# Attention in a two-block transformer kernel: the probabilities multiplied by the reciprocal of their sum on GpSimd instead of VectorE

## The chip, the cores and the metric

The kernel runs on one core of a Trainium2 chip. The metric is the device time of one execution in microseconds. The kernel before was timed three times; the median is 2486.6 us. The profile is of one more execution, with a time of its own.

## What is computed

Everything is in float32. A first block has two layers over 256 latent tokens and 256 context tokens of width 1024: modulated norm, one wide input projection, attention with two kinds of heads (six of latent attention with a low-rank key and value, six with a sliding window and a sink), a short convolution, an output projection, and 16 experts. The second block has two layers over the 256 latent tokens with four mixers side by side (stick-breaking attention, RWKV-7, block attention called moba, HGRN-2), gates and a feed-forward part. What matters here is the softmax of the attentions:

```
def sink_softmax(scores, sink):
    s_sink = jnp.broadcast_to(sink..., scores.shape[:-1] + (1,))
    p = jax.nn.softmax(jnp.concatenate([scores, s_sink], axis=-1), axis=-1)
    return p[..., :-1]
...
    s = (einsum('bqhd,bkhd->bhqk', qn, kn) + einsum('bqhr,bkr->bhqk', qr, kr)) * MLA_SCALE
    p = jax.nn.softmax(s, axis=-1)
    return jnp.einsum('bhqk,bkhd->bqhd', p, v)
```

In layer 0 both token streams attend (12 heads each); in layer 1 the latent one only. Latent queries see 512 keys (context and latent), context queries see 256. In each layer of the second block moba has four heads with 256 keys, all causal.

## The kernel before, in words

Five engines run programs of their own, in order, and meet at semaphores. `Signals.mark` counts an event on a semaphore of the engine that makes it, and `at` gives the value that another engine must wait for; the program is built twice, so that the second pass knows all values from the first. TensorE writes to eight PSUM banks, which `take` hands out in turn. Weights stream through a ring of three slots in SBUF, filled by SyncE; a slot is loaded again when TensorE has read it.

All attentions use four functions. A head has 256 queries in two halves j = 0, 1 of 128 rows, so each score tile is 128 x 512 or 128 x 256 (`nk` keys). Buffers alternate by head (`i % 2`). For each head:

- TensorE, `attend_tensor`: `scores(i + 1)`, then `between(i)`, which is filler from elsewhere (in layer 0 the modulation rows of layer 1, L491; in moba the projections of the next columns, L274; nothing in the context stage and in layer 1), then for every second head `values` of two finished heads, then `turned(i - 1)`: it waits for the probabilities of head i - 1 and transposes them (L645), half j = 0 and then j = 1.
- VectorE, `attend_vector`: `stats(i)`: mask if there is one (L679), row maximum (L680), three small operations (L683 to L685); then `normalise(i - 1)`: sum plus sink (L691), reciprocal (L692), the two multiplications of the probabilities (L695), and then `out_turned(i - 1, 1)`, the copy of the second half of the transposed probabilities from PSUM (L610), which waits for TensorE.
- ScalarE, `attend_scalar`: the exponentials with their sums (L720), the sink's exponential (L723), the copy of the first half of the transposed probabilities and of the attended values (L615).
- GpSimd has no part in it. Its program is `sum_pool` (sums of squares for the norms, L551), one memset (L1287) and, in the second block, `rwkv_pool` (L1750, L1755), after each layer's attentions.

Of the kernel before, what the change touches and what calls it, by code (L numbers as in the profile page):

```python
# [16 lines left out]
ALU = mybir.AluOpType  # L17
# [10 lines left out]
L = 2  # L28
# [170 lines left out]
def program(nc, A, out, book):  # L199
    ctx = ExitStack()  # L200
    with ctx:
# [7 lines left out]
        gpsimd = Signals("gpsimd", nc, ctx, book)  # L209
# [13 lines left out]
        stat = sb("stat", 160)  # L223
# [302 lines left out]
        def link(dve, ins):  # L526

            ins.then_inc(*vector.mark("chain"))
            dve.wait_ge(*vector.now("chain"))
# [16 lines left out]
        def sum_pool(pool, T, tag):  # L546

            pool.wait_ge(*scalar.at("squares", tag, 0))
            for k in range(1, KD - 1):
                pool.wait_ge(*scalar.at("squares", tag, k))  # L550
                nc.gpsimd.tensor_tensor(squared(T, tag, 0), squared(T, tag, 0), squared(T, tag, k), ALU.add).then_inc(*gpsimd.mark("summed", tag))  # L551
                pool.wait_ge(*gpsimd.now("summed"))
# [77 lines left out]
        def attend_tensor(pe, heads, prob, probT, tag, between=None):  # L630


            def scores(i):
                q, keys, nk = heads[i][0:3]
                for j in range(2):
                    b = take(pe, "scores", tag, i, j)
                    mm(b[:, 0:nk], q(j), keys, 0, 1).then_inc(*tensor.mark("scores", tag, i, j))

            def turned(i):
                n = heads[i][2] // P  # L640
                for j in range(2):
                    pe.wait_ge(*vector.at("probs", tag, i, j))
                    b = take(pe, "turned_probs", tag, i, j)
                    for k in range(n):
                        last = PE.transpose(b[:, k * P:(k + 1) * P], prob[i % 2][:, j, k * P:(k + 1) * P], ident)  # L645
                    last.then_inc(*tensor.mark("turned_probs", tag, i, j))

            def values(i):

                b = take(pe, "attended", tag, i)  # L650
                for hd in (i, i + 1):
                    for j in range(2):
                        pe.wait_ge(*got("turned_probs", tag, hd, j))
                n = heads[i][2] // P
                for k in range(n):
                    for hd in (i, i + 1):
                        last = mm(b[heads[hd][4], 0:S], heads[hd][3](k), probT[hd % 2][:, k, :], k, n)
                last.then_inc(*tensor.mark("attended", tag, i))

            scores(0)  # L660
            for i in range(len(heads) + 2):
                if i + 1 < len(heads):
                    scores(i + 1)
                if between and i <= len(heads):
                    between(i)
                if i >= 3 and i % 2:
                    values(i - 3)
                if 1 <= i <= len(heads):
                    turned(i - 1)

        def attend_vector(dve, heads, prob, probT, tag, between=None):
            def stats(i):
                nk, mask, sink, scale = heads[i][2], heads[i][6], heads[i][7], heads[i][8]
                mx, nm, es = (stat[:, 32 + 8 * (i % 2) + 2 * n:34 + 8 * (i % 2) + 2 * n] for n in range(3))
                for j in range(2):
                    dve.wait_ge(*tensor.at("scores", tag, i, j))
                    b = bank("scores", tag, i, j)
                    if mask is not None:
                        link(dve, V.tensor_tensor(b[:, 0:S], b[:, 0:S], mask[:, j, :], ALU.add))  # L679
                    V.reduce_max(mx[:, j:j + 1], b[:, 0:nk], AX).then_inc(*vector.mark("chain"))  # L680
                dve.wait_ge(*vector.now("chain"))
                sk = sink.broadcast_to((P, 2))
                link(dve, V.scalar_tensor_tensor(mx, mx, scale, sk, ALU.mult, ALU.max))  # L683
                V.tensor_scalar(nm, mx, -1.0, None, ALU.mult).then_inc(*vector.mark("chain"))
                V.tensor_tensor(es, sk, mx, ALU.subtract).then_inc(*vector.mark("maxima", tag, i))  # L685

            def normalise(i):
                nk = heads[i][2]
                es, sm = (stat[:, 32 + 8 * (i % 2) + 2 * n:34 + 8 * (i % 2) + 2 * n] for n in (2, 3))
                dve.wait_ge(*scalar.at("sink", tag, i))  # L690
                link(dve, V.tensor_tensor(sm, sm, es, ALU.add))  # L691
                link(dve, V.reciprocal(sm, sm))  # L692
                for j in range(2):
                    pr = prob[i % 2][:, j, 0:nk]
                    V.tensor_scalar(pr, pr, sm[:, j:j + 1], None, ALU.mult).then_inc(*vector.mark("probs", tag, i, j))  # L695
                out_turned(i, 1)

            def out_turned(i, j):
                n = heads[i][2] // P
                out_vector(dve, probT[i % 2][:, 0:n, j * P:(j + 1) * P],  # L700
                           bank("turned_probs", tag, i, j)[:, 0:n * P].rearrange("p (k q) -> p k q", k=n),
                           "turned_probs", tag, i, j)

            for i in range(len(heads) + 1):
                if i < len(heads):
                    stats(i)
                if between:
                    between(i)
                if i:
                    normalise(i - 1)  # L710

        def attend_scalar(act, heads, prob, probT, tag, between=None):
            def exps(i):
# [691 lines left out]
        def moba_heads():  # L1405
            causal = C("causal").rearrange("p (a t) -> p a t", a=2)
            heads = []
            for hd in range(4):
                parts, c = sl_of(hd), hd // 2
                heads.append((lambda j, parts=parts, c=c: raw_m[parts, c, j * P:(j + 1) * P], raw_m[parts, 2 + c, :], S,  # L1410
                              lambda k, hd=hd: vt_m[:, k, 64 * hd:64 * hd + 64], parts, ys[2][:, c, :],
                              causal, C("no_sink"), HEAD_SCALE))
            return heads
# [323 lines left out]
        def rwkv_pool(pool, l):  # L1737

            for s in (tensor, scalar, vector):
                value = s.closed(("group1", l))  # L1740
                if value:
                    pool.wait_ge(*value)
            pool.wait_ge(*vector.at("pairs", l, "NT", 1))
            for lev in range(LEVELS):
                if lev:
                    pool.wait_ge(*tensor.at("NT_T", l, lev - 1, 1))
                if lev == 1:
                    pool.wait_ge(level_masked, LEVELS * l + 1)
                    for par in range(2):
                        nc.gpsimd.tensor_tensor(TT[:, par * 512:(par + 1) * 512].rearrange("p (u t) -> p u t", u=4),  # L1750
                                                NL[par].rearrange("p (u t) -> p u t", u=4),
                                                ident.unsqueeze(1).broadcast_to((P, 4, P)), ALU.add).then_inc(identity_added, 1)
                    pool.wait_ge(identity_added, 2 * l + 2)
                for par in range(2):
                    last = nc.gpsimd.tensor_tensor(NL[par].rearrange("p (u t) -> p u t", u=4),  # L1755
                                                   NT[:, par * 512:(par + 1) * 512].rearrange("p (u t) -> p u t", u=4),
                                                   C("levels")[:, lev * P:(lev + 1) * P].unsqueeze(1).broadcast_to((P, 4, P)), ALU.mult)
                last.then_inc(level_masked, 1)
# [477 lines left out]
        with nc.Block() as block:  # L2236
# [84 lines left out]
            @block.gpsimd  # L2321
            def _(pool):
                sum_pool(pool, T2, ("n1", 0))
                for l in range(L):
                    sum_pool(pool, T2 if l < L - 1 else S, ("n2", l))
                    moe_pool(pool, l)
                    sum_pool(pool, T2 if l < L - 1 else S, after_moe(l))
                sum_pool(pool, S, ("m1", 0))
                pool.wait_ge(second_loaded, 16 * len(second_list))
                for l in range(L):  # L2330
                    rwkv_pool(pool, l)
                    sum_pool(pool, S, ("m2", l))
                    sum_pool(pool, S, after_ffn(l))
# [27 lines left out]
```

## Time and profile before

| | |
|---|---|
| median of 3 runs | 2486.6 us (2482.49 to 2492.38) |
| profiled execution | 2477.03 us, its span 2475.3 us |
| TensorE matmul busy | 2245.7 us (91%) |
| VectorE busy | 721.1 us (29%) |
| ScalarE busy | 452.8 us (18%) |
| GpSimd busy | 99.0 us (4%) |
| mean granted TensorE clock | 0.969 |

The span runs from the first to the last instruction of the profiled execution. Busy shares are means over stages that have different limits; TensorE's busy time contains modelled ends of pipelined matmuls. The attention stages lie at 229 to 308 us (latent tokens, layer 0), 310 to 353 (context tokens, layer 0), 827 to 902 (latent tokens, layer 1), and near 1290 to 1311 and 1908 to 1931 (moba).

### The profile page before, as it was taken

The page shows a single profiled execution, that of the slowest core. Times are in us where ns is not written, and L with a number is a line of the kernel's source. Part 1 is how long each engine was busy: PE and PEld are TensorE (multiplying, and loading weights), DVE is VectorE, ACT ScalarE, POOL GpSimd, SP SyncE. Part 2 cuts the span into 40 slices and gives each one's busy share as a digit, 9 for nine tenths or more (in the row PEclk, how much of TensorE's full clock was granted, in tenths as well). Part 3 has the DMA queues.
Part 4 walks back from the last instruction along what each step waited for, and adds up shares of the span by engine and source line. Part 5 has one row for each costly group of instructions (what it writes and reads, how often), then busy time and mean ns, then how long its engine had stood idle before and what let it go on. Part 6 is the DMA issues. An engine that isn't in the chain of part 4 may idle for free.

```text
span 2475.3 us, 26852 instructions
## 1 busy us (share of the span) xinstructions
PE 2245.7 (91%) x11495; PEld 1620.3 (65%) x11495; DVE 721.1 (29%) x1521; ACT 452.8 (18%) x973; POOL 99.0 (4%) x97
## 2 busy tenths in 40 slices
PE   5999889999879888888898999999999899999998
PEld 2334344755456465444587888888888778788887
DVE  2106542223232633111345441400014544131001
ACT  3002332111120322000122312100002331120000
POOL 1000001000010000000100110000000011000000
PEclk8999979999999889999999999999999999999999
DMA  9533901599933004999542213334543211244352
GB/s 327 191 135 143 377 1 68 225 409 415 424 147 132 1 34 197 425 422 424 194 140 102 103 44 127 137 136 136 141 146 139 103 69 68 102 147 145 134 137 84
DMA packets 172887, 435.00 MB, mean 176 GB/s; under 512 B 6202, under 2 KB 64482, under 8 KB 156130
## 3 DMA queue, kind: packets, MB, share of 16 engines
q1 hardware_dynamic: 171632, 430.91, 46.8%
q10 hardware_dynamic: 1138, 2.38, 0.3%
q8 instruction: 92, 1.51, 0.3%
q14 instruction: 25, 0.20, 0.0%
HBM read 432.23 MB, written 1.05 MB: 175 GB/s over the span
## 4 chain that ended last, share of the span: by engine, by line
PE 71%; DMA 15%; DVE 8%; ACT 3%; issue 1%; POOL 1%; SPq 0%; ACTq 0%; POOLq 0%; DVEq 0%
PE bank L274 68%; DMA ring<-in_exp_w_up 13%; PE bank L645 1%; DMA ring<-in_w_in 1%; DVE rstd L575 1%; POOL arena L551 1%; PE bank L491 1%; DMA ring<-in_ada_w 1%; DVE stat L680 1%; DVE arena L610 1%; DMA arena<-in_x 1%; DVE bank L625 0%; ACT h L570 0%; ACT arena L615 0%; DVE arena L626 0%
## 5 line engine op out<-in xcount | busy, mean ns | idle before, releaser
L274 PE MATMUL bank<-h,ring 128*128 128x256 f32 (+1 forms) x4064 | 1003.7, 407 | 26.8 <-DMA ring<-in_w_in 10.8
L274 PEld LDWEIGHTS bank<-h,ring 128*128 128x128 f32 x4064 | 771.5, 191 | 245.0 <-issue 125.2
L274 PE MATMUL bank<-arena 128*128 128x128 f32 (+14 forms) x1616 | 314.1, 392 | 47.6 <-ACT arena L615 12.9
L274 PEld LDWEIGHTS bank<-arena 128*128 128x128 f32 (+5 forms) x1616 | 212.5, 206 | 132.8 <-issue 87.3
L274 PE MATMUL bank<-ring,arena 128*64 128x256 f32 x2048 | 234.1, 382 | 48.9 <-DMA ring<-in_exp_w_up 34.1
L274 PE MATMUL bank<-arena,ring 128*128 128x256 f32 x1216 | 264.1, 380 | 6.7 <-DVE arena L2096 3.9
L274 PEld LDWEIGHTS bank<-arena,ring 128*128 128x128 f32 x1216 | 230.7, 190 | 40.1 <-DVE arena L2096 4.7
L274 PEld LDWEIGHTS bank<-ring,arena 128*64 128x64 f32 x2048 | 142.9, 137 | 151.4 <-DMA ring<-in_exp_w_up 47.2
L615 ACT ACTIVATE arena<-bank 128x256 f32<-128x256 f32 (+4 forms) x269 | 119.0, 459 | 637.4 <-PE bank L274 615.0
L610 DVE COPY arena<-bank 128x256 f32<-128x256 f32 (+8 forms) x122 | 65.2, 536 | 389.9 <-PE bank L274 298.8
L551 POOL TENSOR_TENSOR arena<-arena 128x256 f32<-128x256 f32 (+1 forms) x60 | 53.5, 891 | 1877.0 <-ACT arena L544 1875.4
L274 PE MATMUL bank<-ring,h 128*64 128x512 f32 x512 | 116.9, 598 | 3.6 <-DVE h L610 2.4
L544 ACT ACTIVATE arena<-x 128x256 f32<-128x256 f32 (+1 forms) x80 | 36.8, 478 | 341.0 <-DVE x L2175 161.9
L2172 DVE TENSOR_TENSOR arena<-arena,bank 128x512 f32<-128x512 f32 x22 | 15.1, 687 | 285.6 <-PE bank L274 285.6
L1125 DVE TENSOR_TENSOR h<-h,bank 128x256 f32<-128x256 f32 x32 | 13.5, 421 | 254.0 <-PE bank L274 254.0
L274 PE MATMUL bank<-h,arena 128*128 128x256 f32 (+2 forms) x256 | 72.4, 404 | 8.0 <-ACT h L570 5.6
L274 PEld LDWEIGHTS bank<-ring,h 128*64 128x64 f32 x512 | 35.7, 136 | 66.5 <-issue 59.7
L274 PE MATMUL bank<-arena,cst 128*128 128x256 f32 (+1 forms) x132 | 47.8, 492 | 30.6 <-POOL arena L551 21.7
L1144 ACT ACTIVATE arena<-bank 32x512 f32<-32x512 f32 x48 | 28.1, 586 | 242.3 <-PE bank L274 242.1
L615 ACT ACTIVATE h<-bank 128x256 f32<-128x256 f32 (+1 forms) x76 | 30.4, 400 | 210.0 <-PE bank L274 187.1
L720 ACT ACTIVATE arena<-bank,stat 128x512 f32<-128x512 f32 (+1 forms) x88 | 51.1, 586 | 89.9 <-DVE stat L685 89.9
L645 PE MATMUL bank<-cst,arena 128*128 128x128 f32 x272 | 44.1, 302 | 23.1 <-DVE arena L695 21.5
(273 smaller groups left out, 1356.4 us busy)
## 6 DMA issues: line engine op xcount, KB each, us to landing
ring<-in_w_in SPq DMA_DIRECT2D x32, 2048.0 KB, 7.9
ring<-in_exp_w_gate SPq DMA_DIRECT2D x32, 2048.0 KB, 11.0
ring<-in_exp_w_up SPq DMA_DIRECT2D x32, 2048.0 KB, 11.0
ring<-in_exp_w_down SPq DMA_DIRECT2D x32, 2048.0 KB, 10.3
ring<-in_ada_w SPq DMA_DIRECT2D x24, 2048.0 KB, 12.3
ring<-in_w_ffn_down SPq DMA_DIRECT2D x16, 1408.0 KB, 7.0
ring<-in_w_ffn_gate SPq DMA_DIRECT2D x10, 2048.0 KB, 7.8
ring<-in_w_ffn_up SPq DMA_DIRECT2D x10, 2048.0 KB, 7.8
```

Of the source, the lines that this page charges most:

```text
L274: return PE.matmul(o, lhsT, rhs, start=(k == 0), stop=(k == n - 1))
L491: last = PE.matmul(banks[7][g:g + 32, :], cond32[:, k, o:o + 32], w[:, k, :], start=(r == 0 and k < 4), stop=(r == n - 1 and k >= 4))
L544: SC.activation(squared(T, tag, k), x[:, k, 0:T], ACT.Square).then_inc(*scalar.mark("squares", tag, k))
L551: nc.gpsimd.tensor_tensor(squared(T, tag, 0), squared(T, tag, 0), squared(T, tag, k), ALU.add).then_inc(*gpsimd.mark("summed", tag))
L575: link(dve, V.reciprocal(rstd[:, 0:T], rstd[:, 0:T]))
L610: V.tensor_copy(dst, src).then_inc(*vector.mark(*key))
L615: SC.activation(dst, src, func, **kw).then_inc(*scalar.mark(*key))
L645: last = PE.transpose(b[:, k * P:(k + 1) * P], prob[i % 2][:, j, k * P:(k + 1) * P], ident)
L680: V.reduce_max(mx[:, j:j + 1], b[:, 0:nk], AX).then_inc(*vector.mark("chain"))
L720: SC.activation(prob[i % 2][:, j, 0:nk], bank("scores", tag, i, j)[:, 0:nk], ACT.Exp, bias=nm[:, j:j + 1], scale=scale, accum_out=sm[:, j: ...
L1144: last = SC.activation(yst[32 * q:32 * q + 32, g % 2, s, 0:512], bank("expert_down", l, e)[s * CAP:(s + 1) * CAP, :], ACT.Copy)
L2172: V.tensor_tensor(a, a, halves(bank("ffn_up", l, f)), ALU.mult).then_inc(*vector.mark("ffn_up", l, f))
```

## The change

The multiplications of the probabilities leave `normalise` on VectorE, whose reciprocal now marks the event `inverse`. A new function `attend_pool` on GpSimd waits for it and makes the two multiplications of the head. TensorE's transposes wait for GpSimd's event. In GpSimd's program the function stands in front of the sums of norm 2 in the first block, and in front of `rwkv_pool` in the second.

```diff
@@ attend_tensor
-                    pe.wait_ge(*vector.at("probs", tag, i, j))
+                    pe.wait_ge(*gpsimd.at("probs", tag, i, j))
@@ attend_vector
             def normalise(i):
-                nk = heads[i][2]
                 es, sm = (stat[...] for n in (2, 3))
                 dve.wait_ge(*scalar.at("sink", tag, i))
                 link(dve, V.tensor_tensor(sm, sm, es, ALU.add))
-                link(dve, V.reciprocal(sm, sm))
-                for j in range(2):
-                    pr = prob[i % 2][:, j, 0:nk]
-                    V.tensor_scalar(pr, pr, sm[:, j:j + 1], None, ALU.mult).then_inc(*vector.mark("probs", tag, i, j))
+                V.reciprocal(sm, sm).then_inc(*vector.mark("inverse", tag, i))
                 out_turned(i, 1)
@@ new
+        def attend_pool(pool, heads, prob, tag):
+            for i in range(len(heads)):
+                nk = heads[i][2]
+                pool.wait_ge(*vector.at("inverse", tag, i))
+                for j in range(2):
+                    pr, inverse = prob[i % 2][:, j, 0:nk], stat[:, 38 + 8 * (i % 2) + j:39 + 8 * (i % 2) + j]
+                    nc.gpsimd.tensor_scalar(pr, pr, inverse, None, ALU.mult).then_inc(*gpsimd.mark("probs", tag, i, j))
@@ GpSimd's program
                 sum_pool(pool, T2, ("n1", 0))
                 for l in range(L):
+                    for s, tag in enumerate(("lat", "ctx")[0:2 if l < L - 1 else 1]):
+                        attend_pool(pool, head_list(l, s), prob1, (tag, l))
                     sum_pool(pool, T2 if l < L - 1 else S, ("n2", l))
                     moe_pool(pool, l)
...
                 for l in range(L):
+                    attend_pool(pool, moba_heads(), prob_m, ("moba", l))
                     rwkv_pool(pool, l)
```

## Rows read from the trace of the kernel before

**Rows 1.** Page: busy us, share, count; then the chain that ended last

```profile
PE 2245.7 (91%) x11495; PEld 1620.3 (65%) x11495; DVE 721.1 (29%) x1521; ACT 452.8 (18%) x973; POOL 99.0 (4%) x97
...
PE 71%; DMA 15%; DVE 8%; ACT 3%; issue 1%; POOL 1%; SPq 0%; ACTq 0%; POOLq 0%; DVEq 0%
```

**Rows 2.** Stretches: us, busy of PE, PEld, DVE, ACT, POOL, PEclk, DMA, GB/s

```profile
310.00:353.00 43.00, 33.21 (x144) 20.39 (x144) 28.32 (x120) 19.51 (x78) 0.00 (x0) 0.78 0.00 1
...
862.00:876.00 14.00, 11.74 (x43) 6.08 (x42) 8.52 (x24) 4.85 (x16) 0.00 (x0) 0.67 0.00 0
...
980.00:1180.00 200.00, 172.09 (x1174) 93.07 (x1172) 32.77 (x67) 15.65 (x34) 0.00 (x0) 1.00 1.01 424
```

**Rows 3.** TensorE's waits in 310:354, 825:905, 229:308: us in total, times, longest

```profile
PE bank L645 <- DVE arena L695: 8.1, 9, 1.4
...
PE bank L645 <- DVE arena L695: 11.7, 7, 2.3
...
PE bank L491 <- DMA ring<-in_ada_w: 2.4, 1, 2.4
```

**Rows 4.** Timeline, context stage: start us, duration us, engine, line, operation

```profile
334.48 0.17 DVE L692 RECIPROCAL stat<-stat 128x2 f32<-128x2 f32 x1
...
335.08 0.70 PE L645 MATMUL bank<-cst,arena 128*128 128x128 f32 x4 [0.23 <-DVE arena L695]
...
335.82 0.42 DVE L610 COPY arena<-bank 128x256 f32<-128x256 f32 x1 [0.53 <-PE bank L645]
...
337.48 0.17 DVE L692 RECIPROCAL stat<-stat 128x2 f32<-128x2 f32 x1
```

**Rows 5.** Timeline, layer 1's latent stage

```profile
838.34 0.17 DVE L692 RECIPROCAL stat<-stat 128x2 f32<-128x2 f32 x1
...
839.09 1.09 PE L645 MATMUL bank<-cst,arena 128*128 128x128 f32 x8 [1.52 <-DVE arena L695]
...
840.02 3.76 PE L274 MATMUL bank<-arena 96*128 96x512 f32 x20
...
840.22 0.69 DVE L610 COPY arena<-bank 128x512 f32<-128x512 f32 x1 [0.79 <-PE bank L645]
...
849.60 6.38 PE L274 MATMUL bank<-arena 64*128 64x512 f32 x19
```

**Rows 6.** Timeline, where GpSimd follows ScalarE, itself, and TensorE follows it

```profile
377.82 0.63 ACT L544 ACTIVATE arena<-x 128x512 f32<-128x512 f32 x1 [6.24 <-DVE x L941]
...
378.59 1.26 POOL L551 TENSOR_TENSOR arena<-arena 128x512 f32<-128x512 f32 x1 [5.58 <-ACT arena L544]
...
1209.47 5.02 POOL L551 TENSOR_TENSOR arena<-arena 128x256 f32<-128x256 f32 x6 [5.64 <-ACT arena L544]
...
1214.64 0.77 PE L274 MATMUL bank<-arena,cst 128*128 128x256 f32 x1 [5.28 <-POOL arena L551]
...
1356.62 1.27 POOL L1755 TENSOR_TENSOR arena<-arena,cst 128x512 f32<-128x512 f32 x1 [142.12 <-DVE arena L1832]
1357.85 1.27 POOL L1755 TENSOR_TENSOR rstd<-arena,cst 128x512 f32<-128x512 f32 x1
```

**Rows 7.** GpSimd's groups by form: shapes, count, busy us, mean ns, idle before

```profile
L551 POOL TENSOR_TENSOR arena<-arena 128x256 f32<-128x256 f32 x42 | 30.7, 731 | 1188.3 <-ACT arena L544 1187.5
...
L1287 POOL MEMSET arena<- 128x4096 f32 x1 | 3.5, 3511 | 3.5 <-PE bank L274 3.5
...
L2353 POOL MEMSET const-float32-0.0<- 128x1 f32 x1 | 0.1, 98 | 0.2 <-issue 0.2
```

**Rows 8.** Chain in order of time, layer 0: start us, us, what

```profile
266.09 17.15 DMA ring<-in_ada_w
```

**Rows 9.** Timeline, moba of the first mixer layer

```profile
1304.77 0.17 DVE L692 RECIPROCAL stat<-stat 128x2 f32<-128x2 f32 x1
...
1307.24 0.42 DVE L610 COPY arena<-bank 128x256 f32<-128x256 f32 x1 [1.65 <-PE bank L645]
```

## The prediction

> **What bounds the kernel now.** I read the page first. VectorE is busy for 29% of the span and GpSimd for 4%, and the chain of waits puts 71% on TensorE and 8% on VectorE [rows 1]. From that alone the move looks free: VectorE is not the bound and GpSimd has time. So the share is not what to look at, and I went to the stages that hold the edited lines. There are 44 heads in five stretches: 12 latent heads of layer 0 (229 to 308 us), 12 context heads (310 to 353), 12 latent heads of layer 1 (827 to 902), and four moba heads in each of two mixers (near 1290 to 1311 and 1908 to 1931). Then the stages one by one: in the context stage no DMA moves, TensorE is granted 0.78 of its clock and GpSimd is idle; in 14 us of layer 1's stage the same with 0.67 [rows 2]. The table of waits for these stages has the multiplications of L695 first: TensorE waited 8.1 us for them in the context stage and 11.7 us in layer 1's [rows 3].
>
> The timeline of the context stage shows why. It repeats every 3.00 us: reciprocal at 334.48, two multiplications behind it, transposes on TensorE at 335.08 to 335.78, VectorE's copy of them at 335.82, and right behind it the row maxima of the head after next and the next reciprocal, at 337.48 [rows 4]. VectorE is in order and its copy (out_turned) stands in front of the next head's statistics, so reciprocal, multiplication, transposes, copy and maxima form one ring. Whatever is added between reciprocal and copy is added to the ring; TensorE also resumes its scores and values only after the transposes, so the addition counts once, on both sides alike.
>
> **The change, part by part.** It takes 88 multiplications off VectorE (48 of 128x512, 40 of 128x256) and puts as many on GpSimd, with two new crossings between engines. What VectorE saves buys nothing: after the reciprocal its next instruction is the copy that waits for the very transposes, so it merely waits longer. That excludes a gain in these stages. No instruction of another kind is queued on GpSimd in the five stretches: its sums for n2, and rwkv_pool, come after them in its order as they do in time, so its queue delays nothing.
>
> Let *gap* be the time from the start of a head's reciprocal (L692) to the start of its copy (L610). For a head in the ring it is 1.34 us at 256 columns (334.48 to 335.82) and 1.88 at 512 (838.34 to 840.22) [rows 4, 5]. The new gap, if nothing hides it, is: reciprocal 0.17; crossing to GpSimd 0.15; two multiplications of d each, the second starting 0.04 before the first ends, as two unlinked GpSimd operations do at 1356.62 and 1357.85; crossing to TensorE 0.15; the second half of the transposes, 0.35 at 256 (half of 0.70) and 0.50 at 512 (half of 1.09, less the part that overlaps); 0.04 to the copy [rows 4, 5, 6]. The crossings are read where they stand now: ScalarE ends at 378.45 and GpSimd starts at 378.59, GpSimd ends at 1214.49 and TensorE starts at 1214.64 [rows 6]. Hence 0.82 + 2d at 256 columns and 0.97 + 2d at 512. The first multiplications of the pair let the first transposes start earlier, but the second pair ends last for every d above that half.
>
> What is d? No GpSimd operation of one tensor input is in the trace. From below there are memsets, which read nothing: 98 ns for one element and 3511 ns for 4096, so 0.83 ns an element, 0.31 us at 256 and 0.52 at 512. From above there are tensor_tensor operations, which read two: 0.73 us at 256 and 1.27 at 512 [rows 6, 7]. A multiplication by a per-partition scalar reads one, so I take the middle, 0.52 and 0.89 us; VectorE takes 0.35 and 0.48. New gaps: 1.86 at 256 (+0.52 on a ring head) and 2.75 at 512 (+0.87).
>
> Each head loses only what its present gap doesn't already hold. I read the 44 gaps off VectorE's timeline.
> Context, 12 heads: 7 at 1.34 or 1.35, the others 1.59, 1.76, 1.77, 1.98, 2.10. Loss 7 x 0.52 + 0.27 + 0.10 + 0.09 = 4.1 us.
> Layer 1, 12 heads: 7 at 1.87 or 1.88, then 2.17, 2.75, and three of 4.70 to 5.64, where TensorE's own work comes last. Loss 7 x 0.87 + 0.58 = 6.7.
> Layer 0, 12 heads: TensorE has the modulation rows as filler. Five heads have gaps of 3.29 to 7.26 and lose nothing, one has 1.88, six have 2.14 to 2.33. Two of those six (264.57, 276.81) lie in front of the load that TensorE waits for until 283.28: it was issued at 266.09 behind the second set of loads on SP and took 17.15 us, and TensorE stood still for 2.4 us at its end [rows 3, 8], so the 1.1 us that these two lose disappear in that wait. What comes before 258 does not, since the chunk's release, and with it SP's queue, moves along. Loss 1.2 before and 1.9 after: 3.0.
> Moba, 8 heads: gaps 2.47 to 4.92; the tightest is 1304.77 to 1307.24 [rows 9]. The cover is TensorE's 16 projection matmuls (3.7 us) between transposes. Even with d of 0.73 the new gap is 2.28. Loss 0. Without that filler it would be 0.5 us a head.
> The same sum at both ends: with memset prices 2.5 us (0.1 + 1.2 + 1.1), with tensor_tensor prices 29.4 (6.8 + 8.7 + 13.5, 0.4 of the gap before 283 included).
>
> What follows the stages neither returns nor multiplies this. Within them no more than three chunks of weights can be loaded ahead, so later loads shift with the work; the experts behind layer 1 run at 424 GB/s with all DMA engines busy [rows 2] and start their loads as the chunks before are used, so the delay passes to the end.
>
> Sum: 3.0 + 4.1 + 6.7 = +13.8 us. The profiled execution took 2477.0 us with a span of 2475.3, so it would become 2490.8; but it is 9.6 us under the median of the runs shown (2486.6), and on the median's footing the forecast is **2500.4 us**. I give that one.
>
> **The rivals.**
> *The multiplication runs at one element a cycle* (not slower). The memset slope of 0.83 ns an element with the fixed part of the tensor_tensor rows (2 x 0.73 - 1.27 = 0.2) gives d of 0.41 and 0.62, gaps of 1.64 and 2.21, and +4.9 us: 2491.5, no change that can be told. For it: the memset does hold that slope over 4096 elements. Against it: the only arithmetic on GpSimd in the trace needs 2.1 ns an element (0.54 us more for 256 elements more). It decides below 0.85 us for a 128x512 operation, where the sum falls under 12.4 us.
> The Trainium skill ("GPSIMD Engine Reference", § 4.1 Engine selection) has GpSimd about two times slower for two-input elementwise work and says "1-input is roughly line-rate"; the rival above is what this would make here, +4.9 where my middle gives +13.8. By that rule, then, nothing measurable changes. The trace has the two-input case alone, and shows nothing of the other.
> *The multiplication is as slow as tensor_tensor*: +29.4 us, 2516.0. For it: all GpSimd arithmetic here is so. Against it: one operand fewer to read.
> *The clock falls further.* TensorE is at its lower level for part of these stages already. At 849.60 a group of 19 score and value matmuls took 6.38 us where 20 took 3.76 at 840.02 [rows 5]. If the one such group before 849 also falls, that is +3.1, and I allow the context stage, whose groups are smaller, as much again. With the sum: +20, 2506.6. For it: the granted clock of 0.67 and 0.78 in the stages with the ring, against 1.00 among the experts [rows 2]. Against it: the pauses grow by under 1 us each.
> *It doesn't do what it says* would need the multiplications to stay on VectorE or another wait to hold the copy; the diff leaves no room for that, so it has no chance of its own.
>
> **How the numbers follow.** Forecast 0.40 (2493 to 2508 for itself), one element a cycle 0.27, as slow as two inputs 0.12, clock 0.14, something not seen 0.07. A measurement tells about 0.5%, 12.4 us, from no change, so slower begins at 2499. The forecast straddles that: 0.26 of its 0.40 above. With 0.12, 0.13 of the clock's and 0.01 of the rest, slower is 0.52; same 0.44; faster 0.04, all of it from the unseen, since no mechanism here gives time back. The range 2487 to 2514 holds both neighbouring cases and leaves out the very dear multiplication and the free one with a low run.
>
> **What would show each step right or wrong.** The duration of the GpSimd tensor_scalar rows: 0.5 and 0.9 us, or not. The ring of the context stage: 3.5 us instead of 3.0 between reciprocals. In the table of waits TensorE waits for GpSimd at L645, some 15 to 20 us more in total than it did for L695. VectorE's busy time falls by some 35 us (88 multiplications of 0.35 or 0.48), GpSimd's rises by about 64 (48 x 0.89 + 40 x 0.52), and neither matters. The moba stretches keep their length. The prediction is wrong if a 128x512 multiplication takes under 0.7 us, if the crossings are far from 0.15, or if TensorE's granted clock in the layer 1 stage moves by more than a tenth.

## The result: 58 us slower, and the profile after

The changed kernel takes 2545.7 us (median of 4 runs, 2537.6 to 2550.3) against 2488.0 for the kernel before, a ratio of 1.023 with a 95% interval of 1.0196 to 1.0263: +57.7 us where +13.8 was forecast, outside the range. Between the two profiled executions the difference is larger, 69.5 us (2546.6 and 2477.0), because the kernel before was profiled in one of its fastest runs. Where stages are compared below, it is the profiled executions that are compared.

The page of the changed kernel, its chain by engine and three of its groups (columns as before: busy us, mean ns of one, idle before and what ended it):

```profile
PE 70%; DMA 14%; DVE 8%; POOL 3%; ACT 3%; issue 1%; ACTq 0%; POOLq 0%; DVEq 0%
...
L551 POOL TENSOR_TENSOR arena<-arena 128x256 f32<-128x256 f32 (+1 forms) x60 | 53.5, 891 | 1377.1 <-ACT arena L544 1375.5
L715 POOL TENSOR_SCALAR arena<-arena,stat 128x512 f32<-128x512 f32 (+1 forms) x88 | 110.9, 1271 | 657.8 <-DVE stat L691 657.8
...
L645 PE MATMUL bank<-cst,arena 128*128 128x128 f32 x272 | 56.9, 343 | 52.2 <-POOL arena L715 51.7
```

GpSimd has gone from 1% of the chain [rows 1] to 3%, and TensorE's transposes (L645) now wait 51.7 us for it. Its own groups by form give the price that the prediction had to bound:

```profile
L715 POOL TENSOR_SCALAR arena<-arena,stat 128x512 f32<-128x512 f32 x48 | 74.4, 1562 | 431.2 <-DVE stat L691 431.2
L715 POOL TENSOR_SCALAR arena<-arena,stat 128x256 f32<-128x256 f32 x40 | 36.4, 922 | 226.5 <-DVE stat L691 226.5
```

1.56 and 0.92 us, above what was taken for the upper end (1.27 and 0.73). The timeline of the context stage answers to [rows 4]:

```profile
339.60 0.17 DVE L691 RECIPROCAL stat<-stat 128x2 f32<-128x2 f32 x1
339.86 1.82 POOL L715 TENSOR_SCALAR arena<-arena,stat 128x256 f32<-128x256 f32 x2 [12.23 <-DVE stat L691]
...
340.83 0.44 PE L645 MATMUL bank<-cst,arena 128*128 128x128 f32 x2 [1.27 <-POOL arena L715]
...
341.73 0.44 PE L645 MATMUL bank<-cst,arena 128*128 128x128 f32 x2 [0.46 <-POOL arena L715]
...
342.21 0.42 DVE L610 COPY arena<-bank 128x256 f32<-128x256 f32 x1 [2.45 <-PE bank L645]
...
343.87 0.17 DVE L691 RECIPROCAL stat<-stat 128x2 f32<-128x2 f32 x1
```

The gap from reciprocal to copy is 2.61 us (1.34 before), and the next reciprocal comes 4.27 us after the last one (3.00 before): the ring is as described, with another size. The table by stage (us, then busy of PE, PEld, DVE, ACT, POOL, granted clock, DMA, GB/s) shows a second thing; first the kernel before, then the changed one, for layer 0, the context tokens and layer 1:

```profile
235.00:304.00 69.00, 63.06 (x398) 27.48 (x397) 42.20 (x121) 25.40 (x73) 0.00 (x0) 0.97 1.05 381
315.00:351.00 36.00, 27.29 (x127) 15.95 (x125) 25.65 (x112) 17.97 (x72) 0.00 (x0) 0.83 0.00 1
834.00:898.00 64.00, 51.42 (x214) 26.73 (x212) 42.03 (x120) 25.11 (x72) 0.00 (x0) 0.79 0.00 1
```

```profile
236.00:329.00 93.00, 78.29 (x399) 30.14 (x397) 31.82 (x98) 25.79 (x73) 37.23 (x24) 0.81 0.84 300
340.00:392.00 52.00, 38.22 (x124) 20.30 (x124) 18.21 (x84) 18.16 (x72) 21.71 (x24) 0.62 0.00 1
877.00:964.00 87.00, 62.65 (x212) 31.26 (x212) 31.30 (x96) 25.41 (x72) 37.22 (x24) 0.66 0.00 0
```

The stages are 23, 16 and 23 us longer, which is 63 of the 69.5; the work behind them, which starts at the lower clock, makes 5 of the other 7, the time ahead of the first stage 1.0, and moba 0.4. TensorE's granted clock fell from 0.97, 0.83 and 0.79 to 0.81, 0.62 and 0.66. The fourth group of 16 modulation matmuls in layer 0 took 1.9 us and takes 3.6 us in the changed kernel, about twice as long, as at 1.2 instead of 2.4 GHz (timeline of layer 0, before and after):

```profile
245.02 1.92 PE L491 MATMUL bank<-ring,arena 128*32 128x512 f32 x16
```

```profile
249.62 3.64 PE L491 MATMUL bank<-ring,arena 128*32 128x512 f32 x16
```

### The profile page after: what moved, and what is told of

Read it like the earlier page. It is cut to its first block, busy times and chain, and to the rows that moved or that the text cites. A ratio compares the mean times of both kernels' runs of the same rounds, so it can differ in the third digit from the quotient of the medians.

```text
span 2544.8 us, 26855 instructions
## 1 busy us (share of the span) xinstructions
PE 2289.2 (90%) x11495; PEld 1635.6 (64%) x11495; DVE 687.9 (27%) x1433; ACT 453.9 (18%) x973; POOL 209.9 (8%) x185
## 4 chain that ended last, share of the span: by engine, by line
PE 70%; DMA 14%; DVE 8%; POOL 3%; ACT 3%; issue 1%; ACTq 0%; POOLq 0%; DVEq 0%
PE bank L274 67%; DMA ring<-in_exp_w_up 13%; POOL arena L715 2%; PE bank L645 1%; DVE stat L680 1%; PE bank L491 1%; DMA ring<-in_w_in 1%; DVE rstd L575 1%; POOL arena L551 1%; DVE arena L610 1%; DMA arena<-in_x 1%; DVE bank L625 0%; ACT h L570 0%; ACT arena L615 0%; DVE arena L626 0%
## 5 line engine op out<-in xcount | busy, mean ns | idle before, releaser
L274 PE MATMUL bank<-arena 128*128 128x128 f32 (+14 forms) x1616 | 333.0, 409 | 47.7 <-ACT arena L615 12.9
L274 PEld LDWEIGHTS bank<-arena 128*128 128x128 f32 (+5 forms) x1616 | 219.3, 213 | 143.7 <-issue 99.1
L274 PEld LDWEIGHTS bank<-ring,arena 128*64 128x64 f32 x2048 | 143.7, 138 | 152.8 <-DMA ring<-in_exp_w_up 47.9
L715 POOL TENSOR_SCALAR arena<-arena,stat 128x512 f32<-128x512 f32 (+1 forms) x88 | 110.9, 1271 | 657.8 <-DVE stat L691 657.8
L645 PE MATMUL bank<-cst,arena 128*128 128x128 f32 x272 | 56.9, 343 | 52.2 <-POOL arena L715 51.7
L544 ACT ACTIVATE arena<-x 128x256 f32<-128x256 f32 (+1 forms) x80 | 36.8, 478 | 343.5 <-DVE x L2180 161.9
L645 PEld LDWEIGHTS bank<-cst,arena 128*128 128x128 f32 x272 | 36.1, 169 | 85.8 <-POOL arena L715 81.0
```

What stands on the lines that cost most here:

```text
L274: return PE.matmul(o, lhsT, rhs, start=(k == 0), stop=(k == n - 1))
L544: SC.activation(squared(T, tag, k), x[:, k, 0:T], ACT.Square).then_inc(*scalar.mark("squares", tag, k))
L715: nc.gpsimd.tensor_scalar(pr, pr, inverse, None, ALU.mult).then_inc(*gpsimd.mark("probs", tag, i, j))
```

## The experiments

Two causes had to be told apart: the ring (each head pays what GpSimd adds between reciprocal and copy) and the clock (TensorE, idle for longer, runs slower where it does work). All differences are medians against the kernel before, run beside it on the same chip; the ratio's interval tells how far each can be trusted (0.001 is 2.5 us). This table has the length of each stage, from the start of its first reciprocal to the start of its last copy, and the granted clock in it, from the one profiled execution of each run; each experiment below refers to it. In runs 1 and 9 the code of these three stages is that of the kernel before. Its context stage takes 35.7, 37.1 and 36.8 us in the three profiles, and layer 1 64.2, 60.2 and 60.3: single stages differ by up to 4 us without any cause in the code.

| run | us against before | ratio (95%) | layer 0 | context | layer 1 |
|---|---|---|---|---|---|
| kernel before | | | 69.8, 0.97 | 35.7, 0.83 | 64.2, 0.79 |
| changed kernel | +57.7 | 1.023 (1.0196 to 1.0263) | 93.1, 0.81 | 52.0, 0.62 | 87.4, 0.66 |
| 1 moba only | -0.8 | 0.9988 (0.9969 to 1.0007) | 70.0, 0.97 | 37.1, 0.78 | 60.2, 0.83 |
| 2 crossing only | +6.3 | 1.003 (1.0008 to 1.0052) | 69.5, 0.97 | 42.6, 0.66 | 66.3, 0.79 |
| 3 half the columns | +23.3 | 1.0086 (1.0056 to 1.0115) | 70.6, 0.99 | 45.7, 0.66 | 76.6, 0.71 |
| 4 idle matmuls | +48.1 | 1.0182 (1.0147 to 1.0217) | 82.1, 0.96 | 51.6, 1.00 | 85.6, 0.90 |
| 5 fewer idle matmuls | +44.1 | 1.0174 (1.0139 to 1.0209) | 82.0, 0.96 | 51.0, 0.93 | 81.4, 0.90 |
| 6 late copy, GpSimd | -19.8 | 0.9924 (0.9894 to 0.9954) | 70.4, 0.96 | 28.7, 0.94 | 48.6, 0.89 |
| 7 late copy, VectorE | -26.5 | 0.9893 (0.9852 to 0.9934) | 70.4, 0.94 | 29.6, 0.88 | 47.9, 0.93 |
| 8 tensor_tensor form | +25.8 | 1.0108 (1.0076 to 1.0139) | 75.2, 0.93 | 46.3, 0.63 | 78.1, 0.69 |
| 10 late copy, tensor_tensor | -36.2 | 0.9843 (0.9817 to 0.9868) | 68.8, 0.97 | 24.7, 1.00 | 45.1, 0.92 |
| 11 before, idle matmuls | -11.3 | 0.9947 (0.9922 to 0.9972) | 69.7, 0.97 | 35.2, 0.97 | 56.1, 1.00 |
| 12 early maxima, GpSimd | +4.7 | 1.0013 (0.9994 to 1.0031) | 70.6, 0.96 | 42.8, 0.72 | 69.3, 0.76 |

**1. GpSimd multiplies in moba only.** In the first block VectorE keeps its multiplications, and GpSimd's part is taken out there.

```diff
...
-                    pe.wait_ge(*gpsimd.at("probs", tag, i, j))
+                    pe.wait_ge(*(gpsimd if tag[0] == "moba" else vector).at("probs", tag, i, j))
...
```

> Only the eight moba heads are multiplied on GpSimd; the first block multiplies on VectorE as before. Ring theory (each head loses what its gap between reciprocal and copy does not already hold): the tightest moba gap before is 2.47 us and the new one, with two 0.92 us multiplications, 2.61, so at most 0.1 us on each of four heads: +0.5 us over the kernel before. Rival, that GpSimd's work costs by itself (shared memory port, slower neighbours): 16 of 88 multiplications, a fifth of the 57.7 us, +8 to +12 us.

Measured: -0.8 us, no change. Sixteen operations of 0.92 us on GpSimd cost nothing where TensorE's projections lie between the transposes; the 8 to 12 us of the rival are outside the interval.

```profile
L721 POOL TENSOR_SCALAR arena<-arena,stat 128x256 f32<-128x256 f32 x16 | 14.6, 922 | 185.3 <-DVE stat L692 185.3
```

**2. The crossing alone.** GpSimd copies two numbers a row, and VectorE waits for that and multiplies itself; TensorE waits for VectorE.

```diff
...
                 V.reciprocal(sm, sm).then_inc(*vector.mark("inverse", tag, i))
+                dve.wait_ge(*gpsimd.at("probs", tag, i))
+                for j in range(2):
+                    pr = prob[i % 2][:, j, 0:heads[i][2]]
+                    V.tensor_scalar(pr, pr, stat[:, 104 + 2 * (i % 2) + j:105 + 2 * (i % 2) + j], None, ALU.mult)...
...
+                nc.gpsimd.tensor_copy(stat[:, 104 + 2 * (i % 2):106 + 2 * (i % 2)], stat[:, 38 + a:40 + a])...
```

> VectorE multiplies as before, but waits for a GpSimd copy of the two reciprocals (128x2) in between: two crossings and one tiny operation, no long GpSimd work. Ring theory: the gap grows by about 0.09 + 0.1 + 0.09 = 0.3 us, 15 heads pay it whole and some pay part: +4 to +6 us. Rival, that crossings between engines are what is dear: most of the 57.7 us, +30 or more.

Measured: +6.3 us (2 to 13 by the interval), at the upper edge of what the ring gives. In the stage table layer 0 is unchanged and layer 1 has 2 us more, which is within the spread, but the context stage has 7 and its clock fell from 0.83 to 0.66, below the 0.78 of run 1: the shortest gaps there are 1.59 us instead of 1.35, so about 0.24 us more of waiting a head went with the lower clock. Crossings are not what is dear.

**3. Half the columns.**

```diff
-                    pr, inverse = prob[i % 2][:, j, 0:nk], stat[...]
+                    pr, inverse = prob[i % 2][:, j, 0:nk // 2], stat[...]
```

> As the changed kernel, but GpSimd multiplies only the first half of the columns; the other half of the probabilities is left unscaled, so part of the computation is left out. With 2.5 ns an element (0.92 at 256, 1.56 at 512) the operations take 0.92 us for 512 keys and 0.60 for 256, close to the 0.89 and 0.52 of the prediction. Ring theory alone: gaps of 2.83 and 1.97, +16 us (3.4 + 5.2 + 7.4). Ring and clock: the granted clock of the attention stages falls too and adds to it, +20 to +30 us. If the loss were a matter of the count of GpSimd operations and not of their length: the whole 57.7 us.

Measured: +23.3 us, with 14 to 29 by the interval. That is in the range of ring and clock together, but the ring's 16 is inside it too. The run has nearly the prediction's own prices (0.92 and 0.60 us), and its context stage is 10.0 us longer than before where the ring's sum has 5.2, at a clock of 0.66 instead of 0.83; so it points to the clock beside the ring without proving it. What it does show is that the loss follows the length of the operation, not the number of operations.

**4. and 5. Idle matmuls in TensorE's wait, in the changed kernel**, first in run 4, then in run 5. keep_busy(pe, n) issues 2n matmuls of 128x256, which are 4n rows of the profile and take n us at full clock.

```diff
             def turned(i):
                 n = heads[i][2] // P
+                if tag[0] != "moba" and (tag != ("lat", 0) or i % 2):
+                    keep_busy(pe, 1 if tag == ("lat", 0) else 2)
                 for j in range(2):
                     pe.wait_ge(*gpsimd.at("probs", tag, i, j))
```

```diff
+                if tag[0] == "ctx" or tag[0] == "lat" and i % 2:
+                    keep_busy(pe, 2 if tag == ("lat", 1) else 1)
                 for j in range(2):
                     pe.wait_ge(*gpsimd.at("probs", tag, i, j))
```

> The changed kernel with idle matmuls on TensorE in front of its wait for the probabilities in the first block's attentions (four of 128x256 a head in the context stage and in layer 1, two on every second head in layer 0), in time in which it would stand still. Clock theory: the granted clock of 0.63 to 0.82 in these stages rises towards 0.9 and more and some 15 to 25 us of the 57.7 come back: +33 to +43 us over the kernel before. Ring alone: the clock does not matter, the time stays at +58, or rises where the idle matmuls outlast the wait.

> The changed kernel with idle matmuls again, but so few that they end before the probabilities are there: two a head in the context stage, four on every second head in layer 1, two on every second head in layer 0. Ring theory without the clock's part: the losses of the 44 gaps with the measured prices (gaps of 2.61 and 4.11) sum to 12.2 + 12.7 + 18.9 = 44 us, so the time is 42 to 46 us over the kernel before, and layer 0's stage stays at +12. If the clock's share is not what the idle matmuls gave back, it stays near +58 or at the +48 of the run with more of them.

Measured: +48.1 and +44.1 us against the +57.7 of the changed kernel; 48.1 is above the 33 to 43 expected. In run 4 the clock is back (1.00 in the context stage), but four idle matmuls outlast the wait there: its gaps are 3.0 us instead of 2.6. With fewer of them, run 5, the time is the 44 us of the ring's sum. Run 5 by stage:

```profile
237.00:319.00 82.00, 71.88 (x424) 32.91 (x422) 32.00 (x99) 26.38 (x74) 37.28 (x24) 0.96 0.94 340
329.00:379.00 50.00, 37.16 (x166) 22.89 (x166) 17.81 (x83) 17.56 (x70) 21.71 (x24) 0.93 0.00 1
864.00:945.00 81.00, 59.46 (x260) 34.46 (x260) 31.35 (x96) 25.05 (x72) 37.28 (x24) 0.89 0.00 0
```

Layer 0 is 12.2 us longer than before, and the sum of its gaps said 12.2; the context stage 15.3 (12.7; one head there has a gap of 5.04 us, because its idle matmuls ran at the lower clock), layer 1 17.2 (18.9). Adding work to TensorE made the kernel 13.6 us faster (57.7 - 44.1). The intervals of the two ratios overlap slightly, so the size is rough; the three stages are 18.1 us shorter in the profiles. How much of the +57.7 this makes the clock's is taken up in run 11.

**6. and 7. The copy taken out of the ring.** `normalise` no longer ends with out_turned, and the order on VectorE becomes: sum and reciprocal of head k, copy of head k - 1, maxima of head k + 2; once with the multiplications on GpSimd, once on VectorE.

```diff
-                out_turned(i, 1)
...
-            for i in range(len(heads) + 1):
-                if i < len(heads):
+            n = len(heads)
+            for i in range(n + 2):
+                if i < 2:
                     stats(i)
...
-                if i:
-                    normalise(i - 1)
+                if 1 <= i <= n:
+                    normalise(i - 1)
+                if i >= 2:
+                    out_turned(i - 2, 1)
+                if i and i + 1 < n:
+                    stats(i + 1)
```

> The changed kernel with another order on VectorE: sum, reciprocal of head k; the copy of head k-1; then the maxima of head k+2. The copy no longer waits for the multiplication just started, so GpSimd works beside the other engines. Ring theory: what is dear is the place of the multiplication in the ring and not that GpSimd is slow; with the ring open the stages go by the busiest engine, TensorE at 3.7 us a head with 512 keys and 2.1 with 256, GpSimd at 3.15 and 1.85: about 47 us in layer 1 (87 in the changed kernel, 64 before), 27 in the context stage (52, 36), 67 to 70 in layer 0: 20 to 28 us under the kernel before. Rival, that GpSimd's length counts wherever it stands (or that a shared port slows VectorE): the time stays above the kernel before.

> The same order, with the multiplications on VectorE as in the kernel before. VectorE then needs 3.7 us a head (4.4 with a mask) at 512 keys and 2.6 at 256, and is about as busy as TensorE: 10 to 18 us under the kernel before. If GpSimd is a real relief once the ring is open, the run with the multiplications on GpSimd is 5 to 12 us faster than this one; if not, this one is the faster.

Measured: -19.8 and -26.5 us, the first at the edge of the 20 to 28 expected, the second beyond its 10 to 18. With the same 88 slow operations on GpSimd that cost 58 us in the ring, the kernel is 20 us faster than before once the copy does not wait for them: the place in the order made most of the price. The stages of layer 1 (48.6 us) and of the context tokens (28.7) are each under 2 us above the expected 47 and 27. But GpSimd is not shown to be the better place in this form: VectorE has the lower median, and the intervals of the two runs overlap. In run 6 the timeline of layer 1 has the copy (861.56) and the maxima (862.62) of other heads beside the multiplications, which follow each other almost without a pause:

```profile
861.56 0.67 DVE L610 COPY arena<-bank 128x512 f32<-128x512 f32 x1
861.74 3.10 POOL L719 TENSOR_SCALAR arena<-arena,stat 128x512 f32<-128x512 f32 x2 [1.38 <-DVE stat L691]
...
862.62 0.69 DVE L680 TENSOR_REDUCE stat<-bank 128x1 f32<-128x512 f32 x1
...
864.79 1.09 PE L645 MATMUL bank<-cst,arena 128*128 128x128 f32 x8
...
864.95 0.17 DVE L691 RECIPROCAL stat<-stat 128x2 f32<-128x2 f32 x1
...
865.21 3.11 POOL L719 TENSOR_SCALAR arena<-arena,stat 128x512 f32<-128x512 f32 x2 [0.37 <-DVE stat L691]
```

VectorE's copy and maximum, which read PSUM, take 0.67 and 0.69 us beside GpSimd's work and 0.69 and 0.68 in the kernel before, so they are not slowed by it. GpSimd is done with the first pair at 864.84, just as TensorE comes to its transposes, and TensorE waits 4.2 us for GpSimd in the whole stage, 24.5 in the changed kernel's; first run 6, then the changed kernel (us in total, times, longest):

```profile
PE bank L645 <- POOL arena L719: 4.2, 4, 2.9
```

```profile
PE bank L645 <- POOL arena L715: 24.5, 16, 3.4
```

**8. The multiplication as tensor_tensor.**

```diff
-                    nc.gpsimd.tensor_scalar(pr, pr, inverse, None, ALU.mult)
+                    nc.gpsimd.tensor_tensor(pr, pr, inverse.broadcast_to((P, nk)), ALU.mult)
```

> The changed kernel with the multiplication written as tensor_tensor with the reciprocal broadcast along the row, on GpSimd. By the rows of the kernel before a tensor_tensor takes 1.27 and 0.73 us where tensor_scalar took 1.56 and 0.92. Ring theory: gaps of 3.45 and 2.23, about +27 us from the ring and 8 to 15 of clock on top: +33 to +42 over the kernel before, 16 to 24 under the changed kernel. If the form of the operation makes no difference (the broadcast operand costs as much), +58 as before.

Measured: +25.8 us, less than expected, because the form is cheaper still than the tensor_tensor of the kernel before:

```profile
L715 POOL TENSOR_TENSOR arena<-arena,stat 128x512 f32<-128x512 f32 x48 | 48.9, 1041 | 433.3 <-DVE stat L691 433.3
...
L715 POOL TENSOR_TENSOR arena<-arena,stat 128x256 f32<-128x256 f32 x40 | 23.7, 614 | 230.0 <-DVE stat L691 230.0
```

With 1.04 and 0.61 us the shortest gaps are 3.03 and 1.96 and the ring's sum 4.4 + 5.0 + 9.2 = 18.6 us. The rest, 7 us, fits the lower clock of the two later stages (0.63, 0.69), but no run separates it here. Writing the same product in another form brings back more than half of the loss.

**9. Prices on GpSimd.** The kernel before, with more GpSimd operations whose results nobody uses. `a` and `b` are the same part of one tile, so the form with two tensors reads one tile twice.

```diff
+                for w in (128, 256):
...
+                        alone(G.tensor_scalar(a[:, 0:w], a[:, 0:w], c, None, ALU.mult))
...
+                        alone(G.tensor_scalar(a[:, 0:w], a[:, 0:w], 1.0, None, ALU.mult))
...
+                        alone(G.tensor_tensor(a[:, 0:w], a[:, 0:w], b[:, 0:w], ALU.mult))
...
+                        alone(G.tensor_tensor(a[:, 0:w], a[:, 0:w], c.broadcast_to((P, w)), ALU.mult))
...
+                        alone(G.tensor_copy(b[:, 0:w], a[:, 0:w]))
```

> The kernel before with twenty more GpSimd operations on a scratch tile behind its first sums, one after another, results unused; GpSimd is idle there and nothing waits for them. It measures prices at 128x128 and 128x256: tensor_scalar with a per-partition operand, tensor_scalar with a constant, tensor_tensor with two tensors, tensor_tensor with the operand broadcast along the row, copy. Known: 0.92 us for the first and 0.61 for the fourth at 128x256. If the per-partition operand is what makes tensor_scalar dear, the constant form takes 0.6 or less; if the operation itself is (its loop), both take 0.92. The whole time stays at that of the kernel before.

The timeline of GpSimd, with each pair of equal operations merged (by pointer, by constant, two tensors, broadcast, copy), and the one row of VectorE that lies beside the second half:

```profile
29.60 1.31 POOL L2334 TENSOR_SCALAR scratch<-scratch 128x128 f32<-128x128 f32 x2
31.00 1.14 POOL L2336 TENSOR_SCALAR scratch<-scratch 128x128 f32<-128x128 f32 x2
32.23 0.88 POOL L2338 TENSOR_TENSOR scratch<-scratch 128x128 f32<-128x128 f32 x2
33.18 0.88 POOL L2340 TENSOR_TENSOR scratch<-scratch 128x128 f32<-128x128 f32 x2
34.12 0.64 POOL L2342 COPY scratch<-scratch 128x128 f32<-128x128 f32 x2
34.87 1.95 POOL L2334 TENSOR_SCALAR scratch<-scratch 128x256 f32<-128x256 f32 x2
36.90 2.25 POOL L2336 TENSOR_SCALAR scratch<-scratch 128x256 f32<-128x256 f32 x2
39.24 2.10 POOL L2338 TENSOR_TENSOR scratch<-scratch 128x256 f32<-128x256 f32 x2
41.42 1.96 POOL L2340 TENSOR_TENSOR scratch<-scratch 128x256 f32<-128x256 f32 x2
```

```profile
36.95 6.97 DVE L579 TENSOR_TENSOR h<-x,rstd 128x512 f32<-128x512 f32 x8
```

At 128x128 the order is plain (one operation, without the short pause between the two): 0.60 us by pointer, 0.53 by constant, 0.40 for both tensor_tensor forms, 0.29 for a copy. The operation itself is the dear thing, and the pointer adds only 0.08. The first 128x256 pair, by pointer, is still undisturbed, 0.92 us each as in the changed kernel. From 36.95 on VectorE runs operations on two SBUF tensors, and the 128x256 rows beside them are no clean prices: tensor_tensor with a broadcast takes 0.94 us there and 0.61 in run 8. That half shows interference between the two engines instead, and in both directions. The same eight operations of VectorE take 4.90 us in the kernel before, where GpSimd does nothing, and 6.97 beside the probe; single ones go from 0.68 to 1.1 us beside GpSimd's tensor_tensor. The kernel before:

```profile
37.56 4.90 DVE L578 TENSOR_TENSOR h<-x,rstd 128x512 f32<-128x512 f32 x8
```

(The run's single time, 2474.2 us, says nothing finer than that the probe is nearly free.)

**10. Late copy and the cheaper form.** The edits of 6 and 8 together.

> The changed kernel with the late copy on VectorE and the cheaper form on GpSimd (1.04 and 0.61 us instead of 1.56 and 0.92). If GpSimd's length still holds the open pipeline back, this is 3 to 8 us faster than the late copy with tensor_scalar, and reaches or passes the one that multiplies on VectorE: 22 to 30 us under the kernel before. If TensorE bounds the open pipeline, it is the same as the first, 20 under.

Measured: -36.2 us, the best of all, 16 us under the late copy with tensor_scalar, where 3 to 8 were expected. The context stage went from 28.7 to 24.7 us with its clock at 1.00 instead of 0.94, layer 1 from 48.6 to 45.1. So GpSimd's length did still hold the open pipeline back; the part of the clock in that is not separated. Against the late copy on VectorE (0.9893, 0.9852 to 0.9934) it is probably ahead, but the intervals overlap.

**11. Idle matmuls in the kernel before.** Two on every second head of the context stage and of layer 1.

> The kernel before with two idle matmuls on every second head of the context stage and of layer 1's attention, in TensorE's wait for the probabilities. If its own granted clock of 0.83 and 0.79 in these stages costs time, they rise to 0.9 and more and 3 to 7 us come back. Ring theory without clock: no change, within 0.2%.

Measured: -11.3 us, more than expected. Its windows of the two stages:

```profile
317.00:352.00 35.00, 30.30 (x150) 18.15 (x149) 25.56 (x111) 17.29 (x71) 0.00 (x0) 0.97 0.00 1
833.00:889.00 56.00, 46.08 (x237) 25.80 (x236) 41.96 (x121) 24.76 (x72) 0.00 (x0) 1.00 0.00 1
```

Layer 1's attention went from 64.2 us (60.2 in run 1) to 56.1 with the clock at 1.00. The kernel before was paying for its clock already. That changes how run 5 is to be read, which has the clock held up and was compared with a kernel that has not. With idle matmuls in both, runs 5 and 11, the change costs 44.1 + 11.3 = 55.4 us, and the three stages are 12.3, 15.8 and 25.3 us longer, 53.4 in all. The lower clock takes about as much from the kernel before (11.3) as from the changed one (13.6), and the difference between these two is far below the noise. So nearly the whole +57.7 is what longer gaps cost with the clock held up.

**12. Only the maxima out of the ring**, on the changed kernel: reciprocal k, maxima of head k + 2, copy k.

```diff
-                out_turned(i, 1)
...
-                if i < len(heads):
+                if i < 2:
...
                 if i:
                     normalise(i - 1)
+                    if i + 1 < len(heads):
+                        stats(i + 1)
+                    out_turned(i - 1, 1)
```

> The changed kernel with the order reciprocal k, maxima of head k+2, copy k: the maxima hide behind GpSimd's multiplication, but the copy still waits for it, so reciprocal, multiplication, transposes and copy stay a ring. Ring theory by its sum: about 5.0 us a head at 512 keys (6.6 in the changed kernel, 4.3 before) and 3.3 at 256 (4.3, 3.0): layer 0 at 70, context stage 39, layer 1 about 60 to 64 us, in all between 5 under and 8 over the kernel before. Rival, that any order which lets the maxima go first opens the pipeline as the late copy does: 20 under.

Measured: +4.7 us, within the ring's -5 to +8 and far from the 20 under of an open pipeline; the stages of 42.8 and 69.3 us are a little above the 39 and 60 to 64 expected, at clocks of 0.72 and 0.76. A ring is only as short as all that stands in it: taking the maxima out and leaving the copy is not enough.

## Why the prediction was wrong

*The structure was right.* The ring of reciprocal, multiplication, transposes, copy and maxima, the rule that a head loses what its gap doesn't already hold, and the 44 gaps held: with the measured gaps of 4.11 and 2.61 the same sum is 12.2 + 12.7 + 18.9 = 43.8 us. Run 5, with the clock held up, measured +44.1; how near that comes is partly luck, since the kernel it is compared with ran at its lower clock for part of these stages. The like comparison is run 5 against run 11: by the gaps of run 11 the sum is 12.4 + 13.2 + 24.2 = 49.8 us, measured are 53.4, and the gap of 5.04 us in run 5 makes 2.4 of the difference. Moba cost nothing, as said (its tightest gaps went from 2.5 to 2.6 us).

*The term that was mis-sized is d.* The prediction took 0.89 and 0.52 us, the middle between memset and tensor_tensor, and measured are 1.56 and 0.92. That is 43.8 instead of 13.8, 30 of the 44 us that were missing. Run 8, with 1.04 and 0.61 us, got 32 us back. What failed is the assumption that time goes by the number of tensors read, with tensor_tensor as the upper end: run 9 has tensor_scalar at 0.60 and tensor_tensor at 0.40 us for 128x128. The upper bound was a row of another operation, not a bound.

*The crossings* were put at 0.15 us each and are 0.09 in (339.77 to 339.86) and 0.05 out (341.68 to 341.73). This took 0.16 us a head off, in the other direction. The second half of the transposes gave most of it back at 256 columns, 0.44 us instead of 0.35, so the formula with the true d gives 2.66 and 4.09 where 2.61 and 4.11 are measured. (The sum at memset prices comes to 1.8 and not to the 2.5 us that stand in the prediction; nothing rests on it.)

*The clock* was a rival at 0.14 and +6 us beside the forecast's ring, and the prediction's own sign came: in layer 1 the granted clock moved by more than a tenth, from 0.79 to 0.66. It is real, and idle matmuls give 13.6 us back. But they gave 11.3 back in the kernel before as well, so it is no price that only the changed kernel pays. The step that failed beside d is that the gaps of the kernel before were taken as fixed. Three of layer 1's, 4.70 to 5.64 us, were allowed to hold the whole multiplication because TensorE's own work ends last there; it ended late because it ran at the lower clock, and in run 11 no gap of that stage is over 2.36. The remaining 14 us, 57.7 less 43.8, can be read either way: as clock lost anew by the changed kernel, or as cover that the slow clock had lent to the sum. The runs don't separate the two. "Against it: the pauses grow by under 1 us each" failed too: with the true d they grow by 1.3 and 2.2 us, and in the context stage about 0.24 us went with a fall from 0.83 to 0.66 (run 2). Run 3, with nearly the predicted d, measured +23.3; its interval, 14 to 29 us, reaches down to the forecast's +13.8, so the forecast might just have held with the right d.

*The line-rate rival* went by the memset's 0.83 ns an element, and for tensor_scalar that is wrong: 0.64 us for 256 elements more is 2.5 ns an element. The Trainium skill, "GPSIMD Engine Reference", § 4.1 Engine selection, says that "1-input is roughly line-rate". For tensor_scalar the trace disagrees, with the 2.5 ns, and the measurement decides.

*That no gain was possible* holds for this order of work: VectorE's 33 us went into waiting.

## What to carry to other kernels

Before an operation is moved to an idle engine, find out whether it stands in a ring, and let whatever else waits in order behind its result go first or later; with the same slow operations the kernel was 58 us slower while the copy waited for them and 20 us faster when it did not. Don't bound the price of one kind of operation by another's row on GpSimd; time the form itself, and try its equivalents. And don't take the gaps of the kernel before as fixed where its granted clock is low: a long gap there may be a slow clock and no cover. Compare the granted clock of the stages first, and where two kernels are compared with idle matmuls, put them into both.

## What the runs showed of the hardware that was not expected

On GpSimd a tensor_scalar of 128x512 float32 takes 1.56 us and the equal tensor_tensor with a broadcast second operand 1.04; a tensor_tensor of two full tensors 1.27. VectorE needs 0.48 for the same multiplication.

GpSimd is slowed by VectorE's operations on two SBUF tensors: 0.94 us instead of 0.61 for 128x256 (runs 9 and 8). VectorE is slowed too: eight such operations of 128x512 took 6.97 us beside GpSimd and 4.90 alone (run 9 and the kernel before). VectorE's copies and maxima out of PSUM beside GpSimd kept their 0.67 to 0.69 us (run 6).

Idle matmuls pay: twelve groups of them, 1.0 us each, made the kernel before 11.3 us faster (7 to 19 by the interval), with the granted clock of layer 1's stage going from 0.79 to 1.00 (run 11).
